# mLSTM heads: a head's first states ahead of its scores, numerators in the staging banks, and the next head's rows, queries and exponents inside rounds 5 and 6

## The chip, the core and the metric

The kernel runs on one core of a Trainium2 chip. The metric is the device time of one execution in microseconds (us); lower is better. Below, TensorE (PE in the rows) is the matrix engine, VectorE (DVE), ScalarE (ACT) and GpSimd (POOL) are the other compute engines, and SyncE (SP) issues the transfers from and to the main memory.

## The reference, cut to what matters

The model step has two layers; only the mLSTM mixer of the second is touched. It has NH_C = 4 heads of DH_C = 512, a prompt of 256 tokens whose state starts at zero, and 8 samples of 4 tokens each that carry an old state `C` of 512x512 per head. Per chunk the reference computes:

```
        w_intra = jnp.exp(log_intra - m_t[:, :, None, :]) * jnp.einsum('bthd,bshd->btsh', qc, kc)
        w_inter = jnp.exp(log_inter - m_t)
        num = jnp.einsum('btsh,bshe->bthe', w_intra, vc) + w_inter[..., None] * jnp.einsum('bthd,bhde->bthe', qc, C)
        den = jnp.sum(w_intra, axis=2) + w_inter * jnp.einsum('bthd,bhd->bth', qc, n)
        h = num / jnp.maximum(jnp.abs(den), jnp.exp(-m_t))[..., None]
...
        kw = kc * w_state[..., None]
        C_new = decay[..., None, None] * C + jnp.einsum('bshd,bshe->bhde', kw, vc)
        n_new = decay[..., None] * n + jnp.sum(kw, axis=1)
```

`h` is then divided by its root mean square over the head, scaled by `norm_w`, added to `skip * xc`, multiplied by `silu(z)`, and goes into the down projection.

## The kernel before, in words

The program is one instruction stream per engine, written out by hand; the order on an engine is the order of the code, and engines meet only at semaphores. Between the combined input projection (`IN_C`) and the output projection (`OUT_C`) lies the stage of the four heads.

**Items and rounds.** The old states of a head, 8 samples by two halves (`half`, 256 of the 512 rows), are 16 items of 512 KB; the prompt's new state adds two (`ORDER`, `ITEMS` = 18). A head is `ROUNDS` = 8 rounds (numbered 0 to 7 here) with two items each. In a round TensorE applies the queries to the old states (`old_state`, L2527, summed over the head in PSUM bank 2), forms the outer products of keys and values (`outers`, L2569) in banks 0 and 1 for one item and 4 and 5 for the other, and VectorE makes the new state (`new_state`, L1761: old state times decay plus product). `banks_free` makes TensorE wait until the item that last used the banks is made. Rounds 3 and 4 also hold the prompt's state (`prompt_outer`, L2554, copied out by ScalarE in `prompt_state`, L1141).

**Transfers.** SyncE's queue runs through the items in order: `c_store(i)` waits until item i is made and stores it, then `c_load(i + 8)` waits for the store that frees the slot (10 slots, `cring`) and loads. Nearly everything is 512 KB per transfer: 34 per head (16 loads, 18 stores).

**The rest of the head** is spread over the rounds by `chunk(h, b)`, one such function on each of TensorE, ScalarE and VectorE, called after the states of round b. Products of one head that are soon read pass through two staging banks (6 and 7) in the order of `USES`: `staged(h, name)` on TensorE waits until the use two places earlier was read (`stage_read_a` for ScalarE's reads, `stage_read_v` for VectorE's, listed in `DVE_READS`). Before the change:

- round 0: `denominators` (L2483 to L2488) and `numerators` (L2499, L2500) on TensorE; absolute value and the Silu of `z` on ScalarE; maximum, reciprocal and the division `hT` on VectorE (L1822 to L1825). The numerators go to banks 4 and 5, so they wait for item 1 of the head and the outer products of round 1 wait for `hT` (`h_ready`).
- round 1: `key_sums` (L2507, L2509, staged as "n"), read by VectorE in `new_n` (L1751, L1752); ScalarE squares `hT` (L1157), GpSimd adds up (`row_sums`).
- round 2: `row_squares` (L2578, "mean"), its root on ScalarE (L1159), reciprocal and `norm_w` on VectorE (L1833, L1835). Round 3: skip and `z` on VectorE (L1843, L1847).
- round 4: the next head's queries (`qk`, L2419, L2423); round 5: its keys (`keys_by_token`, L2431, L2438, `own_keys`, `keys_low`); round 6: its values (`values_by_token`, `values_low` L1706).
- round 7: ScalarE copies bank 2 (`hs4`, L1181), which the next head's first `old_state` overwrites; TensorE broadcasts the next head's gate rows (`head_rows`, L2459, L2460), adds the groups of `hs4` (`sum_groups`, L2536) and forms the next head's `scores` (L2469, L2472). VectorE makes the query copies (`queries`, L1713 to L1723) and the arguments of the exponential (`arguments`, L1728 to L1731), ScalarE the exponentials (`exps`, L1114 to L1116) and the first copy of the own values (`own_values`, `vb`, L1126), VectorE the product with the scores (`weights`, L1738, L1739).

In each round ScalarE's `own_values` makes the values' copy for the next pair of rounds. ScalarE changes its function table three times a head (exponential, Silu, square root). In the last head, which prepares no next one, ScalarE and VectorE split the first two weight tiles of `OUT_C` instead (`act_hi`, `dve_lo`, L710, L1226) in rounds 2 and 3; `OUT_C` begins once the last group sum is copied (`hs_taken`) and turned (`sample_turns`, L2587).

## Time and profile before

| what | value |
|---|---|
| median of 3 runs | 1140.23 us (1136.94 to 1140.27) |
| profiled execution: time / span in the profile | 1140.49 us / 1138.7 us |
| TensorE busy / weight loads / VectorE / ScalarE / GpSimd | 93% / 81% / 58% / 47% / 15% |
| stage of the four heads | from about 645 to 860 us of the span |
| first `old_state` of the four heads | 662.2, 713.6, 764.9, 816.0 us |
| first product of `OUT_C` | 860.1 us |

The profiled execution's own time is 1.8 us above its span (what lies around the first and the last instruction) and 0.3 us above the median. TensorE's busy share over the whole span says little about the heads, which have limits of their own: what counts there is how long one head takes from its first `old_state` to the next head's, and which waits lie in that stretch.

### The profile page before, as it was taken

Reading aid. Unit: us, or ns where it says so; the run is one execution under the profiler, and the core shown is the slowest. Engines: PE = TensorE matmul, PEld = TensorE weight load, DVE = VectorE, ACT = ScalarE, POOL = GpSimd, SP = SyncE. Lnnn points to the kernel's source line nnn. Section 1 sums busy time; section 2 is a strip of 40 time slices with the busy share of each in tenths; the row PEclk is TensorE's granted clock in tenths of the full one; section 3 lists DMA queues with packets and bytes.
Section 4 is the critical chain, followed back from the end, with each engine's and each line's share of the span. In section 5 each row is a group of like instructions: output and inputs, shape, how many; then the busy total and the mean of one; then the engine's idle time right before and its main releaser. Section 6 shows DMA issues by size and latency. Waiting matters only on the chain.

```text
span 1138.7 us, 21640 instructions
## 1 busy us (share of the span) xinstructions
PE 1062.2 (93%) x8479; PEld 922.4 (81%) x8479; DVE 657.3 (58%) x959; ACT 530.7 (47%) x862; POOL 176.2 (15%) x247
## 2 busy tenths in 40 slices
PE   5999999889999999999999988898979999999995
PEld 5987878678999999998899845353528989999995
DVE  5567684623485453336996466768684385544333
ACT  5333655514456553425565345353623457553431
POOL 5124000000104220101401530300000104220100
PEclk9999999998999999999999999999999999999998
DMA  9799897997535555444752149898998535544431
GB/s 350 246 340 344 309 332 282 396 403 276 163 124 167 166 166 163 161 161 129 263 167 94 59 144 407 302 402 311 402 342 331 164 125 166 165 157 161 163 129 42
DMA packets 92762, 261.22 MB, mean 229 GB/s; under 512 B 8934, under 2 KB 10086, under 8 KB 92410
## 3 DMA queue, kind: packets, MB, share of 16 engines
q1 hardware_dynamic: 91818, 258.69, 63.7%
q0 software_dynamic: 432, 1.29, 0.4%
q8 instruction: 55, 0.90, 0.3%
q14 instruction: 25, 0.20, 0.1%
q10 hardware_dynamic: 432, 0.14, 0.0%
HBM read 218.36 MB, written 41.73 MB: 228 GB/s over the span
## 4 chain that ended last, share of the span: by engine, by line
PE 79%; DVE 10%; issue 3%; ACT 3%; DMA 2%; SPq 1%; POOL 0%; DVEq 0%; ACTq 0%; POOLq 0%
PE ps L2059 20%; PE ps L2061 20%; PE ps L2060 20%; DVE cring L1761 2%; PE ps L2171 2%; PE ps L2554 2%; DMA w_raw<-in_weights 1%; PE ps L2569 1%; PE ps L2469 1%; PE ps L2431 1%; PE ps L2527 1%; PE ps L2252 1%; PE ps L2153 1%; PE ps L2419 1%; DVE x L1311 1%
## 5 line engine op out<-in xcount | busy, mean ns | idle before, releaser
L1226 DVE TENSOR_TENSOR w_lo<-w_raw,w_hi 128x1024 fp32r<-128x1024 f32 x232 | 285.2, 1236 | 221.4 <-ACT w_hi L710 220.5
L710 ACT ACTIVATE w_hi<-w_raw 128x1024 fp32r<-128x1024 f32 x232 | 242.4, 1055 | 212.5 <-PE ps L2061 176.8
L2059 PE MATMUL ps<-xin_hi,w_hi 128*128 128x288 f32 x1016 | 305.7, 301 | 17.0 <-DVE w_lo L1226 17.0
L2060 PE MATMUL ps<-xin_lo,w_hi 128*128 128x288 f32 x1016 | 302.8, 298 | 0.0
L2061 PE MATMUL ps<-xin_hi,w_lo 128*128 128x288 f32 x1016 | 302.7, 298 | 0.0
L2059 PEld LDWEIGHTS ps<-xin_hi,w_hi 128*128 128x128 f32 x1016 | 192.3, 189 | 29.1 <-DVE w_lo L1226 18.9
L2060 PEld LDWEIGHTS ps<-xin_lo,w_hi 128*128 128x128 f32 x1016 | 192.1, 189 | 0.7
L2061 PEld LDWEIGHTS ps<-xin_hi,w_lo 128*128 128x128 f32 x1016 | 191.6, 189 | 0.0
L2061 PE MATMUL ps<-hid_hi,w_lo 128*128 128x288 f32 x512 | 152.4, 298 | 0.0
L2060 PE MATMUL ps<-hid_lo,w_hi 128*128 128x288 f32 x512 | 152.3, 297 | 0.0
L2059 PE MATMUL ps<-hid_hi,w_hi 128*128 128x288 f32 x512 | 151.3, 296 | 0.0
L1761 DVE SCALAR_TENSOR_TENSOR cring<-cring,bc,ps 128x1024 f32<-128x1024 f32 x64 | 79.1, 1276 | 30.8 <-PE ps L2569 30.6
L2059 PEld LDWEIGHTS ps<-hid_hi,w_hi 128*128 128x128 f32 x512 | 96.4, 188 | 0.0
L2060 PEld LDWEIGHTS ps<-hid_lo,w_hi 128*128 128x128 f32 x512 | 96.4, 188 | 0.0
L2061 PEld LDWEIGHTS ps<-hid_hi,w_lo 128*128 128x128 f32 x512 | 96.2, 188 | 0.0
L1922 POOL TENSOR_TENSOR hid_lo<-relu,hid_hi 128x288 f32 x64 | 57.2, 896 | 171.5 <-ACT hid_hi L784 171.5
L1321 DVE SCALAR_TENSOR_TENSOR relu<-ps,rstd 128x288 f32<-128x288 f32 x64 | 29.1, 457 | 73.4 <-PE ps L2061 67.4
L782 ACT ACTIVATE relu<-relu 128x288 f32<-128x288 f32 x64 | 28.3, 442 | 65.0 <-DVE relu L1321 60.3
L1915 POOL TENSOR_TENSOR sqsum<-sqsum,sq 128x288 f32<-128x288 f32 x31 | 25.1, 809 | 162.3 <-ACT sq L770 161.2
L1912 POOL COPY sqsum<-sq 128x288 f32<-128x288 f32 x5 | 2.9, 572 | 298.7 <-ACT sq L770 289.9
L770 ACT ACTIVATE sq<-ps 128x288 f32<-128x288 f32 x32 | 13.2, 412 | 76.5 <-PE ps L2061 76.5
L2569 PEld LDWEIGHTS ps<-vb,kst 64*128 64x128 f32 x128 | 10.4, 192 | 43.6 <-issue 29.7
(413 smaller groups left out, 1658.4 us busy)
## 6 DMA issues: line engine op xcount, KB each, us to landing
w_raw<-in_weights SPq DMA_DIRECT2D x232, 512.0 KB, 3.4
cring<-in_C SPq DMA_DIRECT2D x64, 512.0 KB, 6.4
out_Cs<-cring SPq DMA_DIRECT2D x64, 512.0 KB, 6.9
kv_a<-in_kv SPq DMA_DIRECT2D x52, 448.0 KB, 5.8
kv_b<-in_kv SPq DMA_DIRECT2D x52, 448.0 KB, 6.0
kv_w<-in_kv SPq DMA_DIRECT2D x24, 448.0 KB, 7.6
out_Cp<-cring SPq DMA_DIRECT2D x8, 512.0 KB, 6.6
out_v<-gaqkv SPq DMA_DIRECT2D x1, 1152.0 KB, 12.8
```

The costliest lines, as they stand in the source:

```text
L710: act.activation(w_hi[:, l % UM], w_raw[:, l % W_SLOTS], ACT.Copy).then_inc(hi_ready, 1)
L782: act.activation(relu2[:, l % 2], relu[:, l % 2], ACT.Square).then_inc(relu2_ready, 1)
L1226: dve.tensor_tensor(w_lo[:, l % W_SLOTS], w_raw[:, l % W_SLOTS], w_hi[:, l % UM], ALU.subtract).then_inc(lo_ready, 1)
L1321: dve.scalar_tensor_tensor(relu[:, l % 2], ps[:, bank, 0:T], 0.0, rstd, ALU.max, ALU.mult).then_inc(out_taken, 1)
L1761: dve.scalar_tensor_tensor(cring[s], cring[s], bc[:, h % 2, R_DECAY + b:R_DECAY + b + 1], new, ALU.mult, ALU.add).then_inc(c_new, 1)
L1915: pool.tensor_tensor(sqsum, sqsum, sq[:, m % 2], ALU.add).then_inc(sq_added, 1)
L1922: pool.tensor_tensor(hid_lo[:, bass.ds(m, 1)].rearrange("p a t -> p (a t)"), relu2[:, l], hid_hi[:, bass.ds(m, 1)].rearrange("p a t -> p ( ...
L2059: pe.matmul(out, w_hi[:, j, ws], hi, start=start and kk == 0, stop=False)
L2060: pe.matmul(out, w_hi[:, j, ws], lo, start=False, stop=False)
L2061: last = pe.matmul(out, w_lo[:, l % W_SLOTS, ws], hi, start=False, stop=stop and kk == UK - 1)
L2171: last = pe.matmul(ps[32 * b4:32 * b4 + 32, 4 + c, 0:NK // 2], qz_of[b4][:, h], kv[s][:, c * NK // 2:(c + 1) * NK // 2], start=h == 0, sto ...
L2554: last = pe.matmul(ps[:, banks_of(i) + d, :], ktok[:, tt, es], vw[:, tt], start=tt == 0, stop=tt == 1)
```

## The change

The order within a head is shifted by about one round, in all three `chunk` functions. TensorE does a head's round 0 (`old_state`, `outers`) first and only then `sum_groups` of the head before and this head's `scores`; `denominators` and `numerators` move to round 1, `key_sums` behind the outer products of round 3, `row_squares` to round 4, and `head_rows` of the next head from round 7 to round 5. The numerators are staged as two new uses, `nu0` and `nu1`, in banks 6 and 7, so the semaphores `num_psum` and `h_ready` and their waits are gone. VectorE divides in round 2, updates `n` in round 4, normalises in round 5, applies skip and `z` in round 7 (round 6 in the last head), and makes the next head's queries and exponents' arguments in round 6, ahead of the new states of round 7; the low part of the rows follows in the next head's round 0 (`low_rows`). ScalarE makes the exponentials in round 6, ahead of `own_values` for the next head and of the copy of bank 2 in round 7. Before head 0 the scores are no longer formed. The diff, cut to its core:

```diff
-USES = ["q0", "q1", "q2", "q3", "qo", "kt0", "kt1", "ks", "vt0", "vt1", "vs",
-        "bc0", "bc1", "sc", "n", "mean"]
+USES = ["q0", "q1", "q2", "q3", "qo", "kt0", "kt1", "ks", "bc0", "bc1", "vt0", "vt1", "vs",
+        "sc", "nu0", "nu1", "n", "mean"]
-DVE_READS = ("ks", "vs", "sc", "n")
+DVE_READS = ("ks", "vs", "sc", "nu0", "nu1", "n")
...
         @block.scalar
...
+            def sample_sums_of(h):
+
+                act.wait_ge(hs_sum, h + 1)
+                act.activation(hs[:, h], ps[0:NS, 3, :], ACT.Copy).then_inc(hs_taken, 1)
+                act.wait_ge(hs_taken, h + 1)
+                act.activation(hs_junk, hs[:, h], ACT.Square, accum_out=stok[:, 1, h:h + 1]).then_inc(hs_sq, 1)
             def chunk(h, b):
-                if b == 0:
+                if b == 0 and h:
+                    sample_sums_of(h - 1)
+                if b == 1:
                     act.wait_ge(den_psum, h + 1)
...
-                if b == 1:
-                    act.wait_ge(h_ready, h + 1)
+                if b == 2:
+                    act.wait_ge(stage_read_v, reads(use(h, "nu1"))[1])
                     act.activation(qf[:, :, 0:SEQ], hT, ACT.Square).then_inc(h_sq, 1)
-                if b == 2:
+                    if h + 1 == NH:
+                        act_hi(0, 0, STEP0[OUT_C])
+                if b == 3 and h == 2:
+                    sample_roots(0)
+                if b in (3, 4):
+                    prompt_state(h, b - 3)
+                if b == 4:
                     act.activation(dn, staged(h, "mean")[:, 0:SEQ], ACT.Sqrt, bias=tiny[:, 0:1], scale=1.0 / DH
                                    ).then_inc(stage_read_a, 1)
-                    if h == 2:
-                        sample_roots(0)
-                if b in (2, 3):
-                    if h + 1 == NH:
-                        act_hi(b - 2, 0, STEP0[OUT_C])
-                    prompt_state(h, b - 2)
-                if b == 4 and h + 1 < NH:
-                    qk(h + 1)
+                    if h + 1 < NH:
+                        qk(h + 1)
+                    else:
+                        act_hi(1, 0, STEP0[OUT_C])
                 if b == 5 and h + 1 < NH:
                     keys_by_token(h + 1)
                     own_keys(h + 1)
+                    head_rows(h + 1)
                 if b == 6 and h + 1 < NH:
                     values_by_token(h + 1)
+                    exps(h + 1)
+                if b == 7:
                     if h == 2:
                         sample_high(0)
-                if b == (6 if h + 1 < NH else 4):
+                    act.wait_ge(hs_psum, h + 1)
+                    act.activation(hs4, ps[:, 2, :], ACT.Copy).then_inc(hs_copied, 1)
+                if b == (7 if h + 1 < NH else 6):
                     act.wait_ge(y1_full, h + 1)
                     act.activation(y1_hi[:, ET * h:ET * h + ET, 0:SEQ], hT, ACT.Copy).then_inc(y1_hi_ready, 1)
-                if b == 7:
-                    act.wait_ge(hs_psum, h + 1)
-                    act.activation(hs4, ps[:, 2, :], ACT.Copy).then_inc(hs_copied, 1)
-                    if h + 1 < NH:
-                        head_rows(h + 1)
...
-                    if h + 1 < NH:
-                        exps(h + 1)
...
         @block.vector
...
             def chunk(h, b):
+                last = h + 1 == NH
                 if b == 0:
-
+                    if h:
+                        low_rows(h - 1)
+                    weights(h)
+                if b == 1:
                     dve.wait_ge(den_abs, h + 1)
                     order.after(dve.tensor_tensor(dn, dn, bc[:, h % 2, R_EN:R_EN + SEQ], ALU.max))
                     order.after(dve.reciprocal(dn, dn))
-                    dve.wait_ge(num_psum, h + 1)
-                    dve.tensor_tensor(hT, ps[:, 4:6, :].rearrange("p a (c t) -> p (a c) t", t=SEQ),
-                                      dn.unsqueeze(1).to_broadcast([P, ET, SEQ]), ALU.mult).then_inc(h_ready, 1)
+                if b == 2:
+                    for i in range(2):
+                        src = staged_v(h, f"nu{i}").rearrange("p (c t) -> p c t", t=SEQ)
+                        dve.tensor_tensor(hT[:, 2 * i:2 * i + 2], src, dn.unsqueeze(1).to_broadcast([P, 2, SEQ]), ALU.mult
+                                          ).then_inc(stage_read_v, 1)
                     if h == 2:
                         sample_stats(0)
-                if b == 1:
+                    if last:
+                        dve_lo(0, 0, STEP0[OUT_C])
+                if b == 3 and h >= 2:
+                    sample_folds(h - 2)
+                if b == 4:
                     new_n(h)
...
-                if b == 2:
+                if b == 5:
+                    if not last:
+                        keys_low(h + 1)
                     dve.wait_ge(stage_read_a, reads(use(h, "mean"))[1])
                     order.after(dve.reciprocal(dn, dn))
                     for e in range(ET):
                         order.mark(dve.scalar_tensor_tensor(hT[:, e], hT[:, e], pcol("norm_w", ET * h + e), dn,
                                                             ALU.mult, ALU.mult))
-                    if h + 1 == NH:
-                        dve_lo(0, 0, STEP0[OUT_C])
-                if b == 3:
                     order.wait()
+                    if last:
+                        dve_lo(1, 0, STEP0[OUT_C])
+                if b == 6:
+                    if not last:
+                        values_low(h + 1)
+                        queries(h + 1)
+                        arguments(h + 1)
+                    if h == 2:
+                        sample_rows(0)
+                if b == (6 if last else 7):
+                    if h == 2:
+                        sample_low(0)
                     for e in range(ET):
...
                     dve.tensor_tensor(hT, hT, z[:, ET * h:ET * h + ET, 0:SEQ], ALU.mult).then_inc(y1_full, 1)
...
-                if b == 7:
-                    if h + 1 < NH:
-                        queries(h + 1)
-                        arguments(h + 1)
-                        weights(h + 1)
+                if b == 7 and last:
+                    low_rows(h)
...
         @block.tensor
...
             def numerators(h):
                 pe.wait_ge(stage_read_a, reads(use(h, "vt1"))[1])
-                if h:
-                    pe.wait_ge(h_ready, h)
-                pe.wait_ge(*made(item(h, HALF_B, 0)))
                 for e in range(ET):
-                    out = ps[:, 4 + e // 2, SEQ * (e % 2):SEQ * (e % 2) + SEQ]
+                    if e % 2 == 0:
+                        two = staged(h, f"nu{e // 2}")
+                    out = two[:, SEQ * (e % 2):SEQ * (e % 2) + SEQ]
...
-                last.then_inc(num_psum, 1)
+                    if e % 2:
+                        last.then_inc(stage_full, 1)
...
-                if banks_of(i) and i % ITEMS > 1:
-                    pe.wait_ge(h_ready, i // ITEMS + 1)
...
             def chunk(h, b):
                 if b == 0:
+                    if h:
+                        sum_groups(h - 1)
+                    scores(h)
+                if b == 1:
                     denominators(h)
...
                     numerators(h)
-                if h == 2 and b == 1:
+                if b == 2 and h == 2:
                     sample_turns(0)
...
+                if b == 3:
+                    key_sums(h)
+                if b == 4:
+                    row_squares(h)
+                    if h + 1 < NH:
                         qk(h + 1)
-                    if b == 5:
+                if b == 5:
+                    if h == 2:
+                        sample_scales(0)
+                    if h + 1 < NH:
                         keys_by_token(h + 1)
-                    if b == 6:
-                        values_by_token(h + 1)
-                    if b == 7:
                         head_rows(h + 1)
-                        sum_groups(h)
-                        scores(h + 1)
+                if b == 6 and h + 1 < NH:
+                    values_by_token(h + 1)
...
             for h in range(NH):
                 for j in range(NB):
                     last = old_state(h, j)
...
-                    if j == 1:
-                        key_sums(h)
-                    if j == 2:
-                        row_squares(h)
                     if j in (3, 4):
                         prompt_outer(h, j - 3)
                     outers(h, j)
-                    if h + 1 == NH and j + 1 == NB:
-                        sum_groups(h)
                     chunk(h, j)
+            sum_groups(NH - 1)
```

## Rows read from the trace of the kernel before

**Rows 1.** View by windows: the second head; its header names the columns.

```profile
core 0: us, PE busy (x) PEld busy (x) DVE busy (x) ACT busy (x) POOL busy (x), PEclk, DMA share, GB/s
...
713.60:764.85 51.25, 45.16 (x299) 23.45 (x297) 35.65 (x50) 23.10 (x39) 8.68 (x22) 0.97 0.94 349
```

**Rows 2.** Timeline (start us, us, what), TensorE, last head; then windows, TensorE alone.

```profile
848.47 0.77 PE L2569 MATMUL ps<-vb,kst 64*128 64x512 f32 x4 [2.39 <-DVE cring L1761]
...
core 0: us, PE busy (x), PEclk, DMA share, GB/s
...
709.00:712.30 3.30, 3.30 (x9) 0.51 1.06 410
...
849.00:859.40 10.40, 8.25 (x28) 0.51 1.06 407
```

**Rows 3.** Timeline, TensorE, second head; in brackets idle us before and releaser.

```profile
717.98 0.67 PE L2499 MATMUL ps<-ew,vtk 128*128 128x256 f32 x2 [0.34 <-DVE cring L1761]
...
727.34 0.73 PE L2569 MATMUL ps<-vb,kst 64*128 64x512 f32 x4 [0.98 <-DVE cring L1761]
...
730.08 3.70 PE L2554 MATMUL ps<-vw,ktok 128*128 128x512 f32 x8 [1.01 <-DVE cring L1761]
...
735.05 0.73 PE L2569 MATMUL ps<-vb,kst 64*128 64x512 f32 x4 [1.27 <-issue]
...
737.13 3.70 PE L2554 MATMUL ps<-vw,ktok 128*128 128x512 f32 x8 [0.35 <-DVE cring L1761]
...
759.16 1.05 PE L2536 MATMUL ps<-hs,four_eyes 128*32 128x512 f32 x2 [0.57 <-ACT hs L1181]
```

**Rows 4.** Timeline, TensorE and VectorE, second head: rounds 2, 1 and 4.

```profile
725.66 0.70 PE L2578 MATMUL ps<-qf,ones 128*128 128x256 f32 x2
...
727.27 0.74 DVE L1751 SCALAR_TENSOR_TENSOR nrows<-nrows,dcol,ps 8x512 f32<-8x512 f32 x1
728.03 0.69 DVE L1752 COPY nrows<-ps 1x512 f32<-1x512 f32 x1
...
742.72 2.47 DVE L1761 SCALAR_TENSOR_TENSOR cring<-cring,bc,ps 128x1024 f32<-128x1024 f32 x2 [1.61 <-PE ps L2569]
```

**Rows 5.** Timeline, change to the third head: TensorE, VectorE, then ScalarE.

```profile
755.66 1.04 PE L2527 MATMUL ps<-cring,qz 128*32 128x512 f32 x8
...
757.10 0.69 DVE L1706 TENSOR_TENSOR vst<-ps,vst 128x512 fp32r<-128x512 f32 x1 [2.18 <-ACT vst L1103]
...
761.22 0.28 DVE L1713 TENSOR_TENSOR qn<-qo,bc 128x128 f32<-128x128 f32 x1
...
756.40 0.66 ACT L1103 ACTIVATE vst<-ps,sel 128x512 fp32r<-128x512 f32 x1
...
758.53 0.57 ACT L1181 ACTIVATE hs<-ps 128x512 f32<-128x512 f32 x1
...
763.27 0.51 ACT L1114 ACTIVATE ew<-ew,tokg 128x256 f32<-128x256 f32 x1 [0.39 <-DVE ew L1731]
...
764.19 0.70 ACT L1126 ACTIVATE vb<-vst,sel 128x512 fp32r<-128x512 f32 x1
```

**Rows 6.** Timeline, TensorE: scores for the third and for the fourth head.

```profile
760.13 4.57 PE L2469 MATMUL ps<-qf,xcc 128*128 128x256 f32 x16
...
812.91 2.88 PE L2469 MATMUL ps<-qf,xcc 128*128 128x256 f32 x16
```

**Rows 7.** Timeline, VectorE, second head; page, part 5; timeline, TensorE, last head.

```profile
731.14 1.75 DVE L1833 RECIPROCAL dn<-dn 128x256 f32<-128x256 f32 x1
732.92 1.67 DVE L1835 SCALAR_TENSOR_TENSOR hT<-hT,par,dn 128x256 f32<-128x256 f32 x4
...
738.18 1.67 DVE L1843 SCALAR_TENSOR_TENSOR hT<-xcc,par,hT 128x256 f32<-128x256 f32 x4
739.88 1.22 DVE L1847 TENSOR_TENSOR hT<-hT,z 128x1024 f32<-128x1024 f32 x1
...
L1226 DVE TENSOR_TENSOR w_lo<-w_raw,w_hi 128x1024 fp32r<-128x1024 f32 x232 | 285.2, 1236 | 221.4 <-ACT w_hi L710 220.5
...
844.35 0.73 PE L2569 MATMUL ps<-vb,kst 64*128 64x512 f32 x4 [1.16 <-issue]
...
856.93 1.91 PE L2536 MATMUL ps<-hs,four_eyes 128*32 128x512 f32 x2
```

47 lines of the change are left out of this document (12 added, 35 removed).

## Prediction

> **What bounds the kernel now.** I read the view by windows first, from each head's first old state to the next one's. A head takes 51.25 us [rows 1], TensorE is busy for 45.16 of them and VectorE for 35.65, so TensorE is nearly the bound and its 6.1 us of idle time are what a better order could win. The DMA engines show a share of 0.94 and 349 GB/s over the head [rows 1], and 410 GB/s at a share of 1.06 where they are saturated [rows 2]. 34 transfers of 0.524 MB at 410 GB/s are 43.5 us: the transfers, too, would allow a shorter head, but they are not what the head waits for at 51. Next the timeline of TensorE: in the second head I want to see each gap and its releaser. 0.34 before the numerators, 0.98 before round 2's outer products, 1.01, 1.27 and 0.35 around the prompt's products, 0.57 before the group sum [rows 3]. None is long. The rest of the argument is to lay the new order of each engine over the same durations and see which waits come out.
>
> **What the change takes away, per head.** Numerators in the staging banks no longer wait for item 1: 0.34. Round 2 no longer has its outer products behind the key sums on VectorE: 0.98. VectorE's new_n leaves round 1 too, so that the new states of round 2 are ready sooner: about 0.5 of the 1.01, and the 0.35. The group sum comes after round 0 and finds its copy ready: 0.57 [rows 3]. Together 2.7 us. No product is removed: `scores`, the group sum and the gate rows are moved, not saved. The division in two halves instead of one instruction costs VectorE about 0.1 us and nothing on the path.
>
> **What it adds, first wait: the next head's queries.** q0 comes two uses after "n" in the staging order, so TensorE may write it only when VectorE has read "n". That read moves from round 1 to round 4, behind both new states of that round, while `qk` still stands right after that round's outer products. VectorE needs 2.47 for the two states, then 0.74 and 0.69 [rows 4], 3.9 us, and some 0.2 us for the two handoffs (I take them from the gaps between an end and the start it releases). TensorE has only the square sums, 0.70 [rows 4], in between. It stands for 3.4 us. Before, the read lay three rounds earlier. Queued behind the wait are all of `qk`, round 5 and so the rest of the head.
>
> **Second wait: the copy of bank 2.** The next head's first old state overwrites bank 2, so it waits for ScalarE's copy `hs4`. ScalarE runs in order, and the copy now stands behind `exps` and `own_values` of the next head; `exps` waits for VectorE's `arguments`, these for `queries` and `values_low`, and that for ScalarE's copy of the values. The chain, from the end of the value products, where round 7's old states begin (755.66) [rows 5]: ScalarE's copies end at 757.06, 1.40; `values_low` 0.6 to 0.7; `queries` and `arguments` 2.05 (761.22 to 763.27); exponentials 0.92 (763.27 to 764.19); own values about 0.6 to the next start; the copy 0.57 [rows 5]; handoff 0.1. That is 6.3 us. TensorE has for it only round 7's old states, 1.0, and outer products, 0.67. It stands for 4.6 us. The old order covered the same chain with the gate rows, the group sum and the scores (4.57 [rows 6]); these now lie elsewhere. VectorE's new states of round 7 queue behind this chain, but they end inside the wait.
>
> **Third wait: the gate rows.** bc1 needs the bank of "ks", which VectorE's `keys_low` frees after ScalarE's copy. By the values' copy and subtraction of the same shape (0.66, 0.69 [rows 5]) and 0.4 of handoffs that is 1.75 us after the keys, of which the first gate row covers 1.0, as the group sum's product of the same width [rows 3]: 0.8 us.
>
> So a head gains 2.7 and loses 8.8: 6.1 us longer, 57.3 instead of 51.25. Three heads have a successor: **+18.3 us**.
>
> **Other moved work.** VectorE's normalisation (1.75 and 1.67 [rows 7]) moves ahead of round 6's new states, which delays them by about 1.5 us; the value products of the next head, which follow on TensorE, cover that. Skip and z (1.67, 1.22 [rows 7]) and the low rows lie beside the group sum and scores of the next head. SyncE's queue waits for the same items in the same order, later by up to 3 us, with loads 8 items ahead; at 57 us a head instead of 43.5 the transfers have slack, so I cost it at nothing. If a head fell below 44 us that cover would be gone. GpSimd's diagonals start on the same signal as before, and its square sums have from round 2 to round 4. The table loads are as many as before.
>
> **The ends.** Head 0 starts its states without the scores and head 3 takes scores and one group sum in: 5.5 out, 5.5 in, zero. In the last head the 2.2 us of removed waits are gained up to round 4. After that VectorE is the path: from the end of round 4's outer products it has new states 2.4, new_n 1.45, new states 2.4, normalisation 3.4, a weight split 1.24, new states 2.4, skip and z 2.9 [rows 4, 7], 16.2 us; then ScalarE's high part of the rows (1.0, in front of the copy in its queue), the copy 0.6, handoffs: the last group sum starts 18.0 us after round 4. Before it is 11.9 us (845.08 to 856.93 [rows 7]). 6.1 less 2.2 is **+3.9 us**.
>
> **TensorE's clock.** Rows first: a gap of 2.39 us in the last head's round 6 is followed by a granted clock of 0.51 from 849.0 to 859.4 [rows 2], that is 1.2 instead of 2.4 GHz, while the gaps of up to 1.27 us [rows 3] have none behind them. There is one stretch of 3.3 us at 0.51 at the head change already [rows 2]; it lies in the scores, which take 4.57 us there and 2.88 at full clock [rows 6], 1.7 us each time. The two new gaps of 3.4 and 4.6 us are both longer than 2.39, so I expect a slow stretch behind each: one more per head, at 1.7 us: **+5.1 us**. The Trainium skill, TensorE: Matmul & The Clock Gate, section Part 1: The HAM clock gate, says the same against this change, that the default state is throttled and activity releases it; by that rule a group of products behind any long idle time starts at half rate, and the sum stays as it is, while without it the sum would be 5.1 lower.
>
> **The sum.** 18.3 + 3.9 + 5.1 = 27.3 us. Profiled execution before 1140.5 (its span 1138.7 and 1.8 around it, 0.3 above the median of 1140.2): **1167.8 us**, 2.4% slower. Bounds: no slow stretch at all, not even those of today, takes off the 5.1 and another 5.1: 1158 and a little under. Two more slow stretches per head than I count, and one before the output projection, add 5.1 to 7: 1175. Handoffs doubled (some 1 us a head) add 3.
>
> **Rivals.** (1) Both waits bind, but the clock is no worse than now, because the slow stretches only move from the scores to the products behind the gaps: 1140.5 + 22.2 = 1162.7. For it: only one stretch per head is seen today although there are many small gaps. Against it: the gap of 2.39 us. Chance 0.25. (2) One of the two long waits does not bind, say because ScalarE's copy is reached sooner than I chain it: 3.4 to 4.6 less three times, with its slow stretch: 1149 to 1153. Chance 0.10. (3) Slower still: the gaps make the clock stay low for 10 us as after 849 [rows 2], 5 us per head more: 1180 to 1185. Chance 0.07. (4) The other side: the transfers set the head's time. After the head change the stores stop until round 1 is made, and new states ahead of the scores would keep them going; if the two waits were hidden behind transfers that are slower still, or released early, the head would fall towards TensorE's 45.16 busy us plus the prompt's gaps and the third wait, about 49: 3 x 2.3 less, 1134; at the most 3 x 6.1, 1122. It decides only if the chain of 6.3 us is shorter than 1.7 us, which no row suggests: each of its members waits for the one before. Chance 0.03. (5) Gains and waits cancel, within 3.4 us: needs both waits to be under 2 us together. Chance 0.02. My forecast keeps 0.53.
>
> What a measurement of this kernel can tell from no change is about 0.3%, 3.4 us. Faster 0.03, same 0.02, slower 0.95. The range leaves out rivals 3, 4, 5 and half of 2: 1153 to 1178.
>
> **What would show it.** In the changed profile: the head 57 to 60 us long; q0's first product (L2419 of before) with about 3.4 us of idle before it, released by VectorE's read of "n"; the first old state of heads 1 to 3 with 4 to 5 us of idle, released by ScalarE's `hs4` copy, with the exponentials and own values right ahead of it on ScalarE; no wait for item 1 before the numerators; the DMA share down to about 0.8; PEclk at 0.5 twice per head. TensorE's busy time should grow only by what the clock takes. I am wrong if either gap is under 1 us, or if heads stay at 51 us or less.

## The result and the profile after

The changed kernel takes 1174.49 us (median of 4 runs, 1171.36 to 1178.43) against 1140.25 us for the kernel before beside it: ratio 1.0306 [1.0268, 1.0345], 34 us slower. The profiled execution took 1171.36 us with a span of 1169.6, so 30.9 us over the span before. It is the shortest of the four. The granted clock of the four spans goes from 0.968 down to 0.961: the clock took 37.4 us from the shortest span and 45.9 from the longest (span times one less the clock), which is more than the 7.0 us by which they differ.

First the view by windows, from each first old state to the next one's, then six of the stretches in which TensorE's clock was at half rate (1.2 of 2.4 GHz); the second window below answers to [rows 1].

```profile
core 0: us, PE busy (x) PEld busy (x) DVE busy (x) ACT busy (x) POOL busy (x), PEclk, DMA share, GB/s
656.20:714.50 58.30, 44.65 (x299) 23.99 (x287) 32.78 (x50) 24.11 (x41) 8.64 (x22) 0.93 0.81 276
714.50:773.70 59.20, 47.52 (x295) 24.07 (x295) 35.64 (x52) 23.45 (x38) 8.66 (x22) 0.90 0.89 301
773.70:835.95 62.25, 49.59 (x303) 24.71 (x303) 38.51 (x65) 23.94 (x40) 1.98 (x2) 0.91 0.85 290
835.95:890.90 54.95, 39.84 (x186) 15.75 (x187) 41.19 (x50) 16.56 (x23) 2.87 (x2) 0.81 0.91 323
...
651.90:655.30 3.40, 3.40 (x20) 3.17 (x23) 1.32 (x10) 1.32 (x3) 0.00 (x0) 0.51 0.00 0
689.30:696.10 6.80, 4.93 (x14) 3.58 (x14) 1.68 (x3) 1.64 (x4) 0.00 (x0) 0.51 1.03 378
713.10:719.90 6.80, 5.39 (x15) 1.38 (x16) 6.68 (x9) 3.45 (x7) 0.00 (x0) 0.52 0.94 348
...
799.00:802.40 3.40, 3.40 (x12) 0.67 (x6) 2.85 (x5) 0.01 (x1) 0.00 (x0) 0.54 0.83 266
...
860.20:863.60 3.40, 3.40 (x12) 0.54 (x5) 2.73 (x5) 0.00 (x0) 0.00 (x0) 0.50 1.05 386
877.20:894.20 17.00, 8.43 (x35) 4.68 (x27) 13.57 (x24) 3.15 (x6) 0.00 (x0) 0.50 0.76 257
...
643.20:890.90 247.70, 193.84 (x1191) 98.17 (x1190) 150.65 (x226) 94.72 (x155) 28.85 (x68) 0.89 0.84 288
```

The second head takes 59.20 us instead of 51.25, and VectorE is as busy as it was (35.64 and 35.65). TensorE's idle time is 11.68 us instead of 6.09, and its busy time grew by 2.36 with the same products, at a mean clock of 0.90 instead of 0.97. The last line is the whole stage of the four heads. The same line of the kernel before:

```profile
644.80:860.10 215.30, 185.12 (x1192) 94.66 (x1190) 150.41 (x222) 93.77 (x155) 28.09 (x68) 0.95 0.88 324
```

The stage is 32.4 us longer, 23.7 of it idle time of TensorE (30.2 to 53.9) and 8.7 busy time. Outside it little moved: it starts 1.6 us earlier, and from the first product of the output projection to the end are 278.7 us, as against 278.6.

Where the idle time lies is read in the timeline of TensorE, here round 0 of the first head (659.21), the end of the first head with the change to the second, then the second head's gaps, one gap of the third (797.46), then the last head; the chain on ScalarE and VectorE stands behind it.

```profile
659.21 0.73 PE L2576 MATMUL ps<-vb,kst 64*128 64x512 f32 x4 [2.00 <-ACT vb L1124]
...
687.00 0.70 PE L2585 MATMUL ps<-qf,ones 128*128 128x256 f32 x2
691.17 4.18 PE L2428 MATMUL ps<-xcc,bd_odd 128*128 128x288 f32 x8 [3.47 <-DVE nrows L1755]
...
714.51 1.93 PE L2536 MATMUL ps<-cring,qz 128*32 128x512 f32 x8 [4.53 <-ACT hs L1189]
717.53 1.91 PE L2545 MATMUL ps<-hs,four_eyes 128*32 128x512 f32 x2
719.37 3.29 PE L2478 MATMUL ps<-qf,xcc 128*128 128x256 f32 x16
...
732.76 3.70 PE L2561 MATMUL ps<-vw,ktok 128*128 128x512 f32 x8 [0.43 <-DVE cring L1764]
737.62 0.73 PE L2576 MATMUL ps<-vb,kst 64*128 64x512 f32 x4 [1.16 <-issue]
746.24 0.73 PE L2576 MATMUL ps<-vb,kst 64*128 64x512 f32 x4 [1.16 <-issue]
...
797.46 0.74 PE L2576 MATMUL ps<-vb,kst 64*128 64x512 f32 x4 [2.23 <-issue]
...
868.84 0.73 PE L2576 MATMUL ps<-vb,kst 64*128 64x512 f32 x4 [1.16 <-issue]
...
883.20 1.22 PE L2576 MATMUL ps<-vb,kst 64*128 64x512 f32 x4 [4.75 <-DVE cring L1764]
887.57 1.91 PE L2545 MATMUL ps<-hs,four_eyes 128*32 128x512 f32 x2 [3.15 <-ACT hs L1189]
...
687.08 2.47 DVE L1764 SCALAR_TENSOR_TENSOR cring<-cring,bc,ps 128x1024 f32<-128x1024 f32 x2 [6.14 <-PE ps L2576]
689.58 0.74 DVE L1754 SCALAR_TENSOR_TENSOR nrows<-nrows,dcol,ps 8x512 f32<-8x512 f32 x1
690.33 0.69 DVE L1755 COPY nrows<-ps 1x512 f32<-1x512 f32 x1
...
709.71 0.69 DVE L1709 TENSOR_TENSOR vst<-ps,vst 128x512 fp32r<-128x512 f32 x1 [0.96 <-ACT vst L1101]
...
712.36 0.51 ACT L1112 ACTIVATE ew<-ew,tokg 128x256 f32<-128x256 f32 x1 [1.38 <-DVE ew L1734]
...
713.28 0.70 ACT L1124 ACTIVATE vb<-vst,sel 128x512 fp32r<-128x512 f32 x1
713.89 0.57 ACT L1189 ACTIVATE hs<-ps 128x512 f32<-128x512 f32 x1
```

Both long waits stand where they were forecast, with the chains that were forecast: new states, then both reads for `n`, then the query products (691.17); low values, arguments, exponentials, own values, copy, then the old states (714.51). They recur as 3.47 and 3.52 us, and as 4.53 and 4.85, in the next heads. One more wait, of 2.00 us, was not forecast: the first head's round 0 outer products (659.21) wait for the first copy of the own values. The products behind the two long waits run at half rate: 4.18 us for the eight query products, 1.93 for eight old states, which take 1.04 in [rows 5].

### The profile page after: what moved, and what is told of

The parts are those of the page before. It is cut to its first block, busy times and chain, and to the rows that moved or that the text cites. A ratio compares the mean times of both kernels' runs of the same rounds, so it can differ in the third digit from the quotient of the medians.

```text
span 1169.6 us, 21635 instructions
## 1 busy us (share of the span) xinstructions
PE 1070.7 (92%) x8479; PEld 925.8 (79%) x8479; DVE 657.7 (56%) x963; ACT 530.9 (45%) x862; POOL 176.5 (15%) x247
## 4 chain that ended last, share of the span: by engine, by line
PE 81%; DVE 9%; ACT 4%; issue 3%; DMA 2%; SPq 1%; POOL 0%; DVEq 0%; ACTq 0%; POOLq 0%
PE ps L2068 19%; PE ps L2070 19%; PE ps L2069 19%; PE ps L2561 3%; PE ps L2180 2%; PE ps L2536 2%; PE ps L2576 2%; PE ps L2440 1%; DMA w_raw<-in_weights 1%; DVE cring L1764 1%; PE ps L2428 1%; PE ps L2478 1%; PE ps L2261 1%; PE ps L2518 1%; PE ps L2162 1%
## 5 line engine op out<-in xcount | busy, mean ns | idle before, releaser
L2068 PEld LDWEIGHTS ps<-xin_hi,w_hi 128*128 128x128 f32 x1016 | 192.2, 189 | 27.5 <-DVE w_lo L1229 17.3
L2536 PE MATMUL ps<-cring,qz 128*32 128x512 f32 x256 | 47.0, 669 | 13.9 <-ACT hs L1189 13.9
## 6 DMA issues: line engine op xcount, KB each, us to landing
out_v<-gaqkv SPq DMA_DIRECT2D x1, 1152.0 KB, 12.9
```

The costliest lines, as they stand in the source:

```text
L2068: pe.matmul(out, w_hi[:, j, ws], hi, start=start and kk == 0, stop=False)
L2536: last = pe.matmul(ps[NS * r:NS * r + NS, 2, :], qz_of1(h, HD2 * half + d, b), cring[s][:, d], start=j == 0, stop=j == NB - 1, skip_group_ ...
```

## The experiments

Twelve more kernels were timed. A version is best compared with another by its ratio, since the kernel before beside it took 1140.25 us for the change, 1137.41 for a1 to a4, 1136.61 for c1 and b1 to b3, and 1137.27 for c2 to c4 and d1. The last column of the table is the mean, over a kernel's runs, of the span times one less its granted clock: how much TensorE time the clock took away, an upper bound of what it cost, since in idle time it costs nothing.

| kernel | median us | ratio to before [95%] | span x (1 - clock), us |
|---|---|---|---|
| before | 1137.3 (24 runs, those beside c2 to c4 and d1) | 1 | 17.0 |
| the change | 1174.49 | 1.0306 [1.0268, 1.0345] | 41.9 |
| a1, new_n early | 1158.77 | 1.0194 [1.0166, 1.0222] | 34.4 |
| a2, copy first | 1170.35 | 1.0300 [1.0267, 1.0332] | 38.9 |
| a3, both, and y1_hi late | 1150.89 | 1.0130 [1.0102, 1.0159] | 30.2 |
| a4, the gaps filled | 1168.02 | 1.0287 [1.0253, 1.0320] | 31.5 |
| c1, copy first, normalisation early | 1148.67 | 1.0103 [1.0070, 1.0135] | 27.0 |
| c2, c1 with fills | 1143.86 | 1.0065 [1.0042, 1.0089] | 18.1 |
| c3, c1 with queries late | 1152.82 | 1.0130 [1.0096, 1.0165] | 28.5 |
| c4, c2 and c3 | 1146.05 | 1.0082 [1.0054, 1.0110] | 19.2 |
| b1, before with scores first | 1138.86 | 1.0019 [0.9999, 1.0040] | 18.5 |
| b2, before with numerators staged | 1135.13 | 0.9988 [0.9970, 1.0006] | 16.5 |
| b3, b1 and b2 | 1137.35 | 1.0005 [0.9980, 1.0031] | 18.8 |
| d1, b2 with fills | 1135.67 | 0.9983 [0.9963, 1.0004] | 15.6 |

**a1: the first wait alone.** On the changed kernel, `n` is read one round earlier:

```diff
-                if b == 3 and h >= 2:
-                    sample_folds(h - 2)
-                if b == 4:
-                    new_n(h)
+                if b == 3:
+                    if h >= 2:
+                        sample_folds(h - 2)
+                    new_n(h)
+                if b == 4:
```

> The changed kernel (1174.5 us) with one move: VectorE reads "n" (new_n) in round 3 instead of round 4, so that the bank of the next head's q0 is free when TensorE comes to it. Theory (the two waits and the slow clock behind them each cost what they last): the idle time of 3.47 us before q0 goes in three heads, 10.4 us, and the slow stretch behind it, in which the query products take 3.7 to 4.2 instead of 2.5 us, goes too, another 4: about 1160 us, the heads some 55 us long. Rival A (the bank wait is only the first of two that end together, so another takes its place, say the prompt's copy or a load): less than 5 us won, above 1169. Rival B (waits only, the clock does not follow them): 1164.

Measured 1158.77, 15.7 us below the change; against the kernel before beside each, 21.4 us slower instead of 34.2, 12.9 less. The timeline of TensorE:

```profile
688.54 0.70 PE L2586 MATMUL ps<-qf,ones 128*128 128x256 f32 x2
689.07 2.73 PE L2429 MATMUL ps<-xcc,bd_odd 128*128 128x288 f32 x8
```

The query products follow with no gap, in all three heads, and take 2.73 us instead of 4.18. The waits for the copy stay at 4.53, 4.54 and 4.85. The three gaps were 10.5 us in all, and between the profiled executions the three heads are 11.0 us shorter and the span 11.3 (1158.3); the change's profiled execution is the shortest of its four, this one the longest of its own, which makes the rest of the 15.7. The waits alone account for 10.5; how much the clock gave back, 4 us by the theory and nothing by rival B, these figures (11.3, 12.9, 15.7) do not settle.

**a2: the second wait alone.** ScalarE copies bank 2 ahead of the next head's exponentials:

```diff
                 if b == 6 and h + 1 < NH:
                     values_by_token(h + 1)
-                    exps(h + 1)
                 if b == 7:
-                    if h == 2:
-                        sample_high(0)
                     act.wait_ge(hs_psum, h + 1)
                     act.activation(hs4, ps[:, 2, :], ACT.Copy).then_inc(hs_copied, 1)
+                    if h + 1 < NH:
+                        exps(h + 1)
+                    if h == 2:
+                        sample_high(0)
```

> The changed kernel with ScalarE's copy of bank 2 (hs4) put ahead of the next head's exponentials in round 7. Theory: the chain to the next head's first old state gets shorter by the arguments and the exponentials, so the 4.5 us of idle before it fall to about 2; but VectorE's new states of round 7 still stand behind the queries and arguments and now end last, so the outer products of round 0 wait some 2 us: 1 to 2 us per head won by the waits, and more only if the shorter gaps keep the clock up (2.7 us a head): 1164 to 1171. Rival (the copy was the only thing late): 4.5 us per head and the clock, 3 x 7.2, about 1153. Rival (ScalarE's copy is not what the wait ends on): no change, 1174.

Measured 1170.35, only 4.1 us below the change by the medians, and 1.3 by what each is behind the kernel before beside it (32.9 and 34.2 us), which is not to be told from nothing; yet the wait is cut from 4.5 to 1.82. The timeline of TensorE at the change to the second head:

```profile
712.02 0.73 PE L2577 MATMUL ps<-vb,kst 64*128 64x512 f32 x4
714.58 1.06 PE L2537 MATMUL ps<-cring,qz 128*32 128x512 f32 x8 [1.82 <-ACT hs L1186]
717.59 1.22 PE L2577 MATMUL ps<-vb,kst 64*128 64x512 f32 x4 [1.95 <-DVE cring L1765]
```

1.95 us reappear one step later: the next head's round 0 outer products need banks which VectorE's round 7 new states free, and these queue behind `queries` and `arguments`. The 4.5 us wait had hidden that one, as the forecast said ("they end inside the wait"); with the wait gone it binds. The two together, 3.77 us here and at the next change, are 0.76 less than the 4.53 they replace; at the last change 1.82 and 2.74 replace 4.85.

**a3: both, and the last head's tail.** a1 and a2 together, with `y1_hi` of the last head behind the copy (`if b == 7:` in place of `if b == (7 if h + 1 < NH else 6):`).

> The changed kernel with both moves, and in the last head the copy of bank 2 also ahead of the high part of the rows. Theory: the sum of the two, 14.5 and 5 us, and 2 us in the last head: about 1153 us, still slower than the 1140.2 before, because round 7's new states, the gate rows' wait and VectorE's late normalisation in the last head are left. Rival (the two waits are the whole loss): 1140 to 1145.

Measured 1150.89, 13.5 us above the kernel before beside it instead of 34: 20 are gone. At the change of heads 1.83 us before the first old state and 1.52 to 2.45 before the outer products are left; the tail, in the timeline of TensorE, has become this:

```profile
863.03 1.22 PE L2578 MATMUL ps<-vb,kst 64*128 64x512 f32 x4 [5.29 <-DVE cring L1765]
864.18 1.91 PE L2547 MATMUL ps<-hs,four_eyes 128*32 128x512 f32 x2
```

The wait for the copy (3.15 after the change) is gone, the group sum follows at once, but 5.29 us of wait for VectorE's new states stand ahead of it. So the tail had two holders, one behind the other. The copy behind the high part of the rows in ScalarE's queue held the group sum: it now starts 14.1 us after the end of round 4's outer products (850.12), where in a1, with the same move of `new_n`, it starts 17.3 us after (857.61 to 874.89). What is left, the 5.29 us included, is VectorE's chain.

**a4: what the clock costs.** Products that serve nothing fill the two gaps of the changed kernel; they shorten no wait.

```diff
+                        for _ in range(11 if h < 2 else 0):
+                            pe.matmul(ps[:, 3, 384:512], ones, ident, start=True, stop=True, skip_group_check=True)
                         qk(h + 1)
...
+                if b == 7 and h + 1 < NH:
+                    pe.wait_ge(*reads(use(h + 1, "vt1")))
+                    bank = 6 + use(h + 1, "sc") % 2
+                    for _ in range(16):
+                        pe.matmul(ps[:, bank, 0:P], ones, ident, start=True, stop=True, skip_group_check=True)
```

> The changed kernel with products of constants that nobody reads put into the two gaps: 11 of 128x128x128 before q0 (heads 0 and 1) and 16 before a head's first old state (heads 1 to 3). No wait is changed; TensorE is busy while it waits. Theory (the granted clock falls because TensorE stands still): no stretch at half rate behind the filled gaps, query products at 2.5 us instead of 3.8 or so in two heads, first round and group sum 2.7 us shorter in three: about 10 us won, 1164 to 1166. Rival (the stretches have another cause, or the fill makes the waits longer): 1174 or above, with PEclk at 0.5 where it was.

Measured 1168.02. Windows over the two places, and over the last head's end:

```profile
689.00:696.00 7.00, 5.96 (x41) 4.46 (x43) 3.08 (x4) 2.10 (x6) 0.00 (x0) 1.00 1.03 372
712.00:719.60 7.60, 6.83 (x50) 4.17 (x53) 7.57 (x10) 4.44 (x10) 0.00 (x0) 1.00 0.99 362
872.05:892.45 20.40, 12.19 (x49) 7.69 (x47) 13.88 (x24) 3.15 (x6) 0.00 (x0) 0.50 0.79 278
```

With the gaps filled the clock is 1.00 at both places, where it was 0.51 and 0.52. So it is TensorE's idleness that brings the slow stretches, not the waits as such or the transfers, which are as dense (a share of 1.03). The heads take 56.4, 56.5 and 60.1 us instead of 58.3, 59.2 and 62.3, 6.8 us less. The span is only 3.5 us shorter: the first old state comes 1.1 us later, the last head, whose end has no fills and a still longer slow stretch of 20.4 us, takes 0.9 more, and what follows it 1.3 more. The median is 6.5 us lower, but against the kernel before beside each it is 3.6 (30.6 us behind instead of 34.2), and the two intervals overlap: that the clock stays up at the filled places is shown, what it is worth over the whole kernel only roughly.

**c1: the normalisation off round 5.** Copy first as in a2; `new_n`, the square sums, and the normalisation in round 3, skip and `z` in round 4. On VectorE:

```diff
+                if b == 3:
+                    if h >= 2:
+                        sample_folds(h - 2)
                     new_n(h)
...
-                if b == 5:
...
                     dve.wait_ge(stage_read_a, reads(use(h, "mean"))[1])
...
+                if b == 4:
                     order.wait()
...
+                    dve.tensor_tensor(hT, hT, z[:, ET * h:ET * h + ET, 0:SEQ], ALU.mult).then_inc(y1_full, 1)
                 if b == 5:
                     if last:
                         dve_lo(1, 0, STEP0[OUT_C])
+                    else:
+                        keys_low(h + 1)
```

> The changed kernel with the copy of bank 2 ahead of the exponentials, "n" read in round 3, and the head's own work back in the middle rounds: the square sums behind the key sums in round 3, the normalisation on VectorE in round 3, skip and z in round 4 (instead of rounds 5 and 7, or 6 in the last head). Theory (what is left of the loss after both moves lies in VectorE's late work, above all in the last head, where the outer products of round 7 wait 5.3 us): that gap falls to about 2 us and the wait of the last group sum goes, 6 us, and some 0.5 us per head at the head change: about 1144 us where the version with both moves took 1150.9 and the kernel before 1137.4. Rival (the last head is bound by its transfers, so VectorE's order there does not matter): 1150 again.

Measured 1148.67, 4.7 us above the 1144 that was expected: in the last head the waits for VectorE's new states are now 1.58, 3.50 and 0.72, 5.80 in all, where a3 had 7.83 (0.95, 1.59 and 5.29), and at the changes of heads 1.83 stays with 1.10, 1.95 and 2.74. But the clock took 27.0 us from it, and 16.4 from the kernel before beside it: 10.6 us more, which could be up to that much of the 12.1 us that it is behind. The next run tests that.

**c2: c1 with fills.** 7 fill products ahead of each next head's first old state (the second loop of a4, with 7 for 16), 5 and 13 ahead of the outer products of the last head's rounds 5 and 6:

```diff
+                    if h + 1 == NH and j in (5, 6):
+                        for _ in range(5 if j == 5 else 13):
+                            pe.matmul(ps[:, 3, 384:512], ones, ident, start=True, stop=True, skip_group_check=True)
                     outers(h, j)
```

> The version with the copy ahead and the normalisation early, plus products that serve nothing in three of its gaps: 7 before the first old state of heads 1 to 3 (gap of 1.83 us), 5 and 13 before the outer products of the last head's rounds 5 and 6 (1.58 and 3.50 us). They carry nothing and shorten no wait. Theory (what is left of its 1.0% over the kernel before is TensorE's clock, as its mean span less the time lost to the granted clock is 1119.9 us, and 1118.5 for the kernel before): half-rate time in the stage falls from 33.5 us to about 20, TensorE has some 7 us less to do, and 5 to 7 us come off: 1142 to 1144, ratio about 1.005. Rival (the stage is held by VectorE's chain, and the clock only makes TensorE wait less): within 2 us of 1148.7.

Measured 1143.86, within what the theory gave: 6.6 us behind the kernel before beside it, where c1 was 12.1 behind. In the profiled executions what was won lies at the end: from the fourth head's first old state to the turning of the last sums c2 takes 49.2 us and c1 50.9, and from there to the end of the span 277.7 and 279.7, as c1's slow stretch of 13.7 us (from 858.6) reaches into the output projection; the first three heads take 158.7 us in both, so the fills at the changes of heads won nothing in these two executions. The clock now takes 18.1 us, practically as before the change, so the 6.6 us have another cause. The timeline at the change to the second head:

```profile
706.56 1.83 PE L2641 MATMUL ps<-ident,ones 128*128 128x128 f32 x14
708.47 1.06 PE L2538 MATMUL ps<-cring,qz 128*32 128x512 f32 x8
711.48 0.73 PE L2578 MATMUL ps<-vb,kst 64*128 64x512 f32 x4 [1.95 <-DVE cring L1766]
```

The 1.83 us are filled, not gained. The waits that the fills only cover are counted in c1: over the stage, to the turning of the last sums, TensorE is idle for 35.5 us there and for 30.2 in the kernel before, and these 5.3 us are most of the 6.6. By stretches, each up to the next head's round 0 outer products: 0.8 less ahead of the first head; 2.4 more in the first (2.00 of them the wait for the own values, as at 659.21), 1.4 in the second (7.43 against 6.05) and 2.3 in the third; in the last head as much as before.

**c3: queries and arguments behind round 7's new states**, to remove the 1.95:

```diff
                     if not last:
                         values_low(h + 1)
-                        queries(h + 1)
-                        arguments(h + 1)
...
+                if b == 7 and not last:
+                    queries(h + 1)
+                    arguments(h + 1)
```

> The version with the copy ahead and the normalisation early; the next head's queries and arguments moved on VectorE from ahead of round 7's new states to behind them. Theory (the gap of 1.10, 1.95 and 2.74 us before the next head's round 0 outer products, released by VectorE's new states, comes from the 2.1 us of queries and arguments ahead of these): the three gaps go, the 1.83 us ones ahead of the first old states stay, the scores do not wait: 5 us less, about 1143.5. Rival (the queries and exponentials are then late for the scores and the weights): a new gap of 1 us or more before the scores or the denominators in each head, and no gain.

Measured 1152.82, 15.6 us behind the kernel before where c1 was 12.1 behind; the two intervals overlap, but no gain is left of the 5 us expected. Neither theory nor rival had it right; the timeline, TensorE, then VectorE:

```profile
710.08 1.83 PE L2539 MATMUL ps<-cring,qz 128*32 128x512 f32 x8 [4.21 <-issue]
711.85 1.22 PE L2579 MATMUL ps<-vb,kst 64*128 64x512 f32 x4
...
706.22 2.46 DVE L1766 SCALAR_TENSOR_TENSOR cring<-cring,bc,ps 128x1024 f32<-128x1024 f32 x2
708.60 0.28 DVE L1718 TENSOR_TENSOR qn<-qo,bc 128x128 f32<-128x128 f32 x1
...
709.69 0.29 DVE L1728 TENSOR_TENSOR qn<-qn,par 128x128 f32<-128x128 f32 x1
```

The three gaps before the outer products are gone, as wanted. But `queries` also writes `qz`, with which the old states themselves are multiplied, and `old_state` waits for the signal `qs_ready` of its last instruction (709.69): the old states start 0.10 us after that one ended, and the wait of 1.83 has become 4.21 (5.00 ahead of the fourth head). The timeline puts it down to "issue"; the names in the row (out<-cring,qz) and the code tell it. In this order VectorE owes TensorE two things at once: the queries for round 0's old states, and the new states that free banks for round 0's outer products. Whichever goes second is late. Only the whole of both blocks was moved; the queries ahead of the new states with the arguments behind them was not tried.

**c4: both edits.**

> Both of the two edits on the same version. Theory (they act on different gaps): their gains add, about 1138, ratio 0.999 to 1.003, that is the change's reordering with its three waits taken out brings nothing over the kernel before, since what it wins in waits is under 3 us a head and the tail takes 3 to 4 of it. Rival: the last head's VectorE chain holds 4 us more, 1142 or above.

Measured 1146.05, 6.8 us below c3: the number of the rival, but not through the last head's chain; 2.45, 2.45 and 3.24 us of the `qz` wait are left beside the fills. The fills are worth 6.8 us here over c3, beside the same runs of the kernel before and with no run of the one among those of the other (1145.45 to 1148.53, 1150.42 to 1153.31), and 5.5 in c2 over c1.

**b1: on the kernel before, scores ahead of the group sum**, exponentials ahead of `hs_taken`:

```diff
                         head_rows(h + 1)
-                        sum_groups(h)
                         scores(h + 1)
+                        sum_groups(h)
```

> The kernel before with the scores ahead of the group sum in round 7, and the exponentials ahead of the copy of the group sum on ScalarE: the scores cover the wait for the copy of bank 2. Theory: three gaps of 0.57 to 0.88 us go, 2 us; and if the clock at the head change falls because of that gap and the narrow products around it, up to 1.7 us per head more: ratio to the kernel before 0.995 to 0.998. Rival (the clock falls all the same and the group sum comes late for the next head's denominators, which wait for it): ratio 1.000 or a little above.

Measured 1138.86, ratio 1.0019 [0.9999, 1.0040]: nothing won. In its timeline the 0.57 us before the group sum [rows 3] are gone and 1.14 stand before the scores:

```profile
708.79 4.54 PE L2468 MATMUL ps<-qf,xcc 128*128 128x256 f32 x16 [1.14 <-ACT bc L1108]
```

The group sum had covered part of ScalarE's copies of the gate rows.

**b2: on the kernel before, numerators staged**, the part of the change that removes `num_psum` and `h_ready`, alone.

> The kernel before with one part of the change alone: the numerators in banks 6 and 7 as nu0 and nu1, divided in round 0 as before. Theory: that part is harmless and takes away only the wait of 0.34 us for item 1 in each head, 1 us in all: ratio 0.999, not to be told from 1; so the loss of the change lies in the order of the rounds. Rival (the staging banks become the bound, since q0, "n" and "mean" now queue behind the numerators): above 1.003, with idle time before the key sums or the queries.

Measured 1135.13, ratio 0.9988 [0.9970, 1.0006]: harmless, and what it wins (0.34 us a head at most) is not to be told from nothing. **b3, b1 and b2 together:**

> The kernel before with both of the last two edits. Theory: the gains add, 3 us and the clock if it follows: ratio 0.994 to 0.997, a version below both kernels. Rival: no gain, 0.999 to 1.001, since the transfers at 43.5 us a head and TensorE's 45.2 us leave little.

1137.35, ratio 1.0005 [0.9980, 1.0031]: nothing either.

**d1: b2 with fills in the last head**, 8 ahead of round 5's and 4 ahead of round 7's outer products, by the same loop as in c2.

> The kernel before with the numerators staged, plus products that serve nothing in the last head: 8 in the gap of 2.39 us before round 5's outer products and 4 in the 1.51 us before round 7's. Theory (the slow stretch of about 10 us that follows that gap in the kernel before costs TensorE products at half rate, on the path): the stretch at 845 to 860 is gone in the profile; against the same kernel without them 2 to 4 us less, about 1132, ratio 0.996. Rival (VectorE's new states are the bound in those rounds, and TensorE's slow products hide behind them): within 1 us of 1135.1, ratio 0.999.

Measured 1135.67, ratio 0.9983 [0.9963, 1.0004], where b2 alone had 0.9988: the number of the rival. The windows of d1:

```profile
846.00:850.80 4.80, 2.60 (x19) 0.94 (x18) 4.15 (x4) 0.00 (x0) 0.00 (x0) 0.99 1.05 401
850.80:857.60 6.80, 6.18 (x24) 2.69 (x22) 3.22 (x3) 0.60 (x1) 0.00 (x0) 0.51 1.06 410
```

The fills kept the clock only until 850.8, and a gap of 1.79 for VectorE's new states stayed ahead of round 6's outer products. But this does not show that slow products cost nothing there, for the fills hardly changed the clock: over its runs it took 15.6 us from d1 and 16.5 from b2, and b2's own profile has only 3.4 us at half rate in its last head (from 845.5), behind the same gap of 2.39 us that is followed by 10.4 us in [rows 2]. No version was found that is faster than the kernel before by more than the measurement can tell.

## Why the prediction was right

Forecast 1167.8 us, range 1153 to 1178, measured 1174.5. Of the 6.7 us between, 3.1 lie between the profiled execution (1171.4) and the median. By its steps, in the profiled executions:

| step | forecast | measured |
|---|---|---|
| waits removed, second head | 2.7 | 2.9: 0.34, 0.98, 0.57 and 0.35 gone, 1.01 to 0.43, 1.27 to 1.16 |
| wait for "n" | 3.4 | 3.47, 3.47, 3.52 |
| wait for the copy of bank 2 | 4.6 | 4.53, 4.53, 4.85 |
| wait of bc1 | 0.8 | 0.54 |
| net idle time, second head | +6.1 | +5.6 |
| last head: round 4's outer products to the group sum | 18.0 | 18.0 |
| idle time of TensorE, stage | +22.2 | +23.7 |
| busy time of TensorE, stage (the clock) | +5.1 | +8.7 |

**The waits** were right to 0.3 us each, and a1 and a2 show each with its cause: move the read of `n` and the first is gone; move the copy and the second falls to 1.8. The third wait is smaller since its handoffs took less: from the end of the key products (701.34) to the second gate row (702.93) are 1.59 us, with copy and subtraction for 1.44 of them, so that 0.15 is left where 0.4 was forecast. That "n" and the copy lie behind other work on engines that run in order is what made both; no product was slower for it, and nothing was added to do.

**The last head** came out as laid: outer products of round 4 end at 869.57 (868.84 and 0.73), the group sum starts at 887.57. a3 shows that both parts of the sum count: VectorE's chain for most of it, and the order of the copy and the high part of the rows on ScalarE, whose change takes 17.3 us down to 14.1.

**The clock** is the term that was mis-sized. The step that failed: "one more per head, at 1.7 us". From 643 to 894 us 57.8 us ran at half rate, and 20.5 before: some 37 us more, and not three stretches of 3.3, 10 in all. Of the six stretches at the gaps of 3.5 and 4.5 us three last 6.8 us, not 3.3; the last head has one of 17.0; and there are stretches that were not counted at all, at 799 and 860, behind idle times of 2.23 and 1.68 us (the forecast took 1.27 as harmless and 2.39 as not, and had nothing between), and at 652 behind one of 0.67. In those 57.8 us TensorE is busy for 44.0, so that at most 22.0 us were lost, and before for 18.5 of the 20.5, at most 9.2 lost. The difference, 12.8, is a bound; TensorE's busy time grew by 8.7, and why by no more, no run shows. The Trainium skill, TensorE: Matmul & The Clock Gate, section Part 1: The HAM clock gate, says that the default state is throttled and that activity releases it; the rows of a4 agree: with the idle time filled the clock is 1.00 at both places. What the clock cost in those runs: 6.8 us in the three heads of a4 with five of the six gaps filled, and 5.5 us in c2, where most of the waits were gone already; the 5.1 in total that was forecast was too little.

Two slips of the forecast lie in this term. The gap of 2.39 us that it places in round 6 stands ahead of round 5's outer products, where d1 has its fills. And its upper bound does not add up: two more stretches in each of three heads and one more, at 1.7 us, are 11.9 us and not 5.1 to 7, which gives 1180 and not 1175.

**The idle time** came out close partly by luck. By stretches it is 0.8 us less ahead of the first head, then 7.5, 5.6 and 6.1 more in the three heads for which 6.1 each was forecast, and 5.3 more in the last, where the 3.9 of the forecast is the gain in length. The first head's 7.5 holds a wait that the forecast put at nothing ("5.5 out, 5.5 in, zero"): with the scores gone from ahead of head 0, its round 0 outer products wait 2.00 us for ScalarE's first copy of the own values (659.21). Every version of the changed order has this wait, and the kernel before does not: there the scores stand between.

**What was not foreseen either**: 1.07 us in the third head, once, which takes 62.25 us where 57 to 60 was forecast. The outer products of round 3 wait 2.23 us (797.46) where their fellows wait 1.16. ScalarE's timeline of the changed kernel:

```profile
793.79 1.06 ACT L1164 ACTIVATE qf<-hT 128x1024 f32<-128x1024 f32 x1 [5.69 <-DVE hT L1839]
794.87 1.28 ACT L1130 ACT_TABLE_LOAD   x1
796.16 0.29 ACT L1130 ACTIVATE stok<-stok,tiny 32x2 f32<-32x2 f32 x1
796.36 1.00 ACT L1139 ACTIVATE cring<-ps 128x1024 f32<-128x1024 f32 x1
```

`sample_roots` now stands ahead of the copy of the prompt's state, with its table load of 1.28 us, and that copy frees the banks. The forecast counted table loads ("as many as before") but not what each stands in front of.

**The rivals.** (1), the clock no worse, fell: TensorE is busy for 8.7 us more in the stage. (2), one wait doesn't bind: both bind, in all three heads. (3), 10 us of slow clock behind each gap, overstated it: 3.4 or 6.8 us, and only in the last head, which has longer waits, 17.0. (4), faster because transfers pace the head, fell: the DMA share of the heads went down from 0.94 to 0.89 [rows 1], and a1 to c2 got faster as their waits went. (5) fell with (2).

**Why even the mended order isn't faster** the forecast had not asked. It took 2.7 us a head as the gain once the waits are gone. In none of a2, a3, c1 and c3 did they all go: with a head's first states ahead of its scores, nothing stands on TensorE between round 7 and the next head's round 0 to cover the copy of bank 2, the queries and the new states. In the kernel before, the gate rows, the group sum (1.05 [rows 3]) and the scores (4.57 [rows 6]) cover all three. c2, the best of the mended versions, is 0.65% slower. That no order with the first states ahead can be faster is not shown.

## What to carry to other kernels

Work between two rounds that looks like an interruption may be the cover of everything the other engines owe at that point; before it is moved, list each thing that the next product waits for and what stands on each in-order engine ahead of it. When one wait is taken away, look for the one that was hidden in it: here 4.5 us became 1.8 and 1.95, and then 4.2. And a new idle time of TensorE costs more than its own length, as the products behind it may run at half rate; filling it with products that serve nothing tells the two apart, and was worth 6.8 us here (c4 over c3).

## What was unexpected of the hardware

TensorE's half rate follows smaller idle times than the forecast took from [rows 2, 3]: stretches of 3.4 us stand behind 1.68 us (860) and behind 0.67 (652), while 1.16 us twice a head, in rounds 3 and 4, mostly had none behind it. The same gap need not bring the same stretch: behind 2.39 us in the last head the profile of the kernel before has 10.4 us at a clock of 0.51 [rows 2], that of b2 3.4. It falls within a longer gap, too: at 713.4, 1.1 us before the old states start. And it may last far longer than the gap: 17.0 us in the last head, in which TensorE works for 8.43.
